# Second block's attention: units of two kinds mixed, heads paired across key groups, scores as three rounded products

## The reference

```python
proj = hn @ w_in                       # q_n, k_c, v_c, k_s, v_s, k_w, v_w, g_n, q_w, k_sw, v_sw
qn = rope(q_n)                         # 8 heads of 64: 2 key groups of 4 heads
k_c, k_s, k_w = rope(...)              # 2 key heads of 64 each
ckv = compress([k_c, v_c])             # 31 compressed keys and values of each key head
o_cmp, p_cmp = compressed_attention(qn, ckv[0], ckv[1], t)
o_slc = selected_attention(qn, k_s, v_s, idx, t)        # all 8 blocks of 64 keys, causal
o_win = banded_attention(qn, k_w, v_w, 512, None)       # 512 of 512 keys: causal
o_nsa = g0 * o_cmp + g1 * o_slc + g2 * o_win; o_nsa = rms_norm(o_nsa)
qw, kw = rope(q_w), rope(k_sw)         # 8 more heads, 2 key groups
o_swa = banded_attention(qw, kw, v_sw, 128, sinks); o_swa = rms_norm(o_swa)
mixed = concat([o_nsa, o_swa]) @ w_out
```

## Time and profile before

| | us |
|---|---|
| median of 3 runs | 1889.32 (1887.1 to 1889.44) |
| profiled execution | 1890.05 |
| its span, first to last instruction | 1888.2 |
| PE busy | 1825.2 (97%) |
| DVE busy | 1332.4 (71%) |
| ACT busy | 975.0 (52%) |

### The profile page before, as it was taken

The page is one execution under the profiler, slowest core; times in us unless marked ns, Lnnn a source line. Parts: engine busy times, 40 slices in busy tenths (PEclk is TensorE's granted clock), DMA queues, the critical chain, the costliest instruction groups (busy, mean ns, idle before and its releaser), DMA issues.

```text
span 1888.2 us, 26991 instructions
## 1 busy us (share of the span) xinstructions
PE 1825.2 (97%) x8975; PEld 1451.8 (77%) x8975; DVE 1332.4 (71%) x1885; ACT 975.0 (52%) x1550; POOL 190.9 (10%) x135
## 2 busy tenths in 40 slices
PE   6999999999999998999999999999898999999998
PEld 5775788888888875688888888887556678888887
DVE  6989777777655899867777755687675567777544
ACT  5468764444433458764444433576665554444322
POOL 0100120000133200020000033200021300000111
PEclk9999999999999999999999999999999999999999
DMA  6220233333233420133333233442000223332332
GB/s 168 71 80 1 65 92 100 93 96 97 77 99 99 109 73 23 33 91 99 90 100 100 72 97 99 109 143 79 12 1 12 78 78 100 91 98 86 89 95 76
DMA packets 285096, 154.46 MB, mean 82 GB/s; under 512 B 16949, under 2 KB 283095, under 8 KB 285015
## 3 DMA queue, kind: packets, MB, share of 16 engines
q1 hardware_dynamic: 284596, 153.26, 28.2%
q10 hardware_dynamic: 419, 0.17, 0.0%
HBM read 151.31 MB, written 2.10 MB: 81 GB/s over the span
## 4 chain that ended last, share of the span: by engine, by line
PE 79%; DVE 9%; issue 6%; ACT 6%; DMA 0%; DVEq 0%; SPq 0%; ACTq 0%
PE bank L575 24%; PE bank L576 24%; PE bank L577 24%; DVE cacc L1770 3%; PE bank L1019 1%; DVE nmax L1837 1%; PE bank L975 1%; PE bank L996 1%; ACT pr L1544 1%; DVE nmax L2071 1%; DVE w_lo L1630 1%; ACT w_hi L1177 1%; ACT pt L1560 1%; DMA x_in<-in_x 0%; PE bank L1091 0%
## 5 line engine op out<-in xcount | busy, mean ns | idle before, releaser
L575 PE MATMUL bank<-h_hi,w_hi 128*128 128x512 f32 x1448 | 571.7, 395 | 6.9 <-DVE w_lo L1630 6.7
L576 PE MATMUL bank<-h_lo,w_hi 128*128 128x512 f32 x1448 | 565.6, 391 | 0.0
L577 PE MATMUL bank<-h_hi,w_lo 128*128 128x512 f32 x1448 | 565.2, 390 | 0.0
L1177 ACT ACTIVATE w_hi<-raw 128x1024 fp32r<-128x1024 f32 (+3 forms) x314 | 312.0, 1000 | 488.2 <-PE bank L577 484.0
L1630 DVE TENSOR_TENSOR w_lo<-raw,w_hi 128x1024 fp32r<-128x1024 f32 (+3 forms) x314 | 375.4, 1201 | 230.9 <-ACT w_hi L1177 230.2
L575 PEld LDWEIGHTS bank<-h_hi,w_hi 128*128 128x128 f32 x1448 | 273.2, 189 | 69.7 <-issue 7.6
L576 PEld LDWEIGHTS bank<-h_lo,w_hi 128*128 128x128 f32 x1448 | 273.4, 189 | 57.8 <-issue 2.2
L577 PEld LDWEIGHTS bank<-h_hi,w_lo 128*128 128x128 f32 x1448 | 273.1, 189 | 57.3
L575 PE MATMUL bank<-a_hi,w_hi 128*128 128x512 f32 x528 | 206.1, 390 | 0.0
L577 PE MATMUL bank<-a_hi,w_lo 128*128 128x512 f32 x528 | 205.5, 389 | 0.0
L576 PE MATMUL bank<-a_lo,w_hi 128*128 128x512 f32 x528 | 205.4, 389 | 0.0
(11 more groups left out here) (317 smaller groups left out, 2258.4 us busy)
## 6 DMA issues: line engine op xcount, KB each, us to landing
raw<-in_w_up SPq DMA_DIRECT2D x132, 512.0 KB, 3.8
raw<-in_w_in SPq DMA_DIRECT2D x39, 512.0 KB, 4.0
raw<-in_w_down SPq DMA_DIRECT2D x48, 384.0 KB, 3.2
raw<-in_w_down SPq DMA_DIRECT2D x48, 320.0 KB, 3.0
raw<-in_w_o SPq DMA_DIRECT2D x16, 512.0 KB, 3.5
raw<-in_cmp_w SPq DMA_DIRECT2D x8, 512.0 KB, 3.9
raw<-in_w_out SPq DMA_DIRECT2D x8, 512.0 KB, 3.4
raw<-in_w_uq SPq DMA_DIRECT2D x8, 288.0 KB, 3.0
```

The source lines that it names most:

```text
L575: mm(o, wh, mh, start=start, stop=False)
L576: mm(o, wh, ml, start=False, stop=False)
L577: return mm(o, wl, mh, start=False, stop=stop)
L1177: last = A_(dst(w_hi), src(raw), ACT.Copy)
```

## The change

- Heads are paired across key groups: pair c holds heads c and c+4, so the two row halves have different key heads. Keys lie once (128 partitions, one add in `rope`), and the q slabs and w_out's slabs are loaded in two DMAs each. The norms' gains, gates, sinks and value columns follow the new pairing.
- Scores: queries and keys are split into high parts (ScalarE, `qk_high`) and low parts (VectorE, `qk_low`), and each unit makes three rounded products on the row halves. `HIGH_SLAB`, `LOW_SLAB`, `HIGH_UNIT` and `LOW_UNIT` place the splits.
- Order: two long units lead, then window units and long units of pairs 0 and 1 alternate; pairs 2 and 3 follow as before. Window chunks and the last long chunk use bank 7, the others bank 6. A sink column is made only when the bank doesn't hold it yet.
- Compressed branch: keys padded from 31 to 32, key heads in a block-diagonal `kcT` and `vcn`: 16 full-array score matmuls instead of 32 on halves, 16 transposes instead of 32, four ScalarE copies instead of eight, one output matmul a unit instead of two.

```diff
-UNITS = nsa_units(0) + nsa_units(1) + [(SC_SWA, c, t) for c in range(PAIRS) for t in range(NT)] + nsa_units(2) + nsa_units(3)
-CHUNKS = [(SC_WIN, 0), (SC_WIN, 1)] + [(SC_SWA, c) for c in range(PAIRS)] + [(SC_WIN, 2), (SC_WIN, 3)]
+def mixed_units(lead):
+
+    nsa, swa = nsa_units(0) + nsa_units(1), [(SC_SWA, c, t) for c in range(PAIRS) for t in range(NT)]
+    pairs = [unit for both in zip(swa, nsa[lead:]) for unit in both]
+    return nsa[:lead] + pairs + swa[len(nsa) - lead:]
+
+
+UNITS = mixed_units(2) + nsa_units(2) + nsa_units(3)
+CHUNKS = [(b, c) for b, c, t in UNITS if t == NT - 1 and b != SC_SLC]
+O_BANK = {chunk: 7 if chunk[0] == SC_SWA or chunk == (SC_WIN, 3) else 6 for chunk in CHUNKS}
...
+def sink_new(u):
+
+    return UNITS[u][0] == SC_SWA and (u < 2 or UNITS[u - 2][:2] != UNITS[u][:2])
...
+HIGH_SLAB = {4: ("ks", 0), 5: ("kw", 0), 6: ("kx", 0), 11: ("qx", 0)}
+LOW_SLAB = {5: ("ks", 0), 6: ("kw", 0), 7: ("kx", 0), 11: ("qn", 0), 12: ("qx", 0)}
+HIGH_UNIT = {4: ("qx", 1), 8: ("qn", 1), 12: ("qx", 2), 18: ("qx", 3), 22: ("qn", 2), 30: ("qn", 3)}
+LOW_UNIT = {5: ("qx", 1), 10: ("qn", 1), 13: ("qx", 2), 19: ("qx", 3), 23: ("qn", 2), 31: ("qn", 3)}
...
+                    load(G2, p, slot(p, KD, P)[:, :, 0:HD2], d_in2[:, :, c:c + HD2])
+                    sp.dma_start(slot(p, KD, P)[:, :, HD2:P], d_in2[:, :, c + PAIRS * HD2:c + (PAIRS + 1) * HD2])\
+                        .then_inc(q2_ready[i - (len(T_ORDER) - 2 * PAIRS)], 16)
...
+                    for c in range(PAIRS):
+                        o = (t % 2 * PAIRS + c) * 2 * NCP
+                        last = mm(C_B[t // 2][:, o:o + 2 * NCP], q_sum[:, 0, c, t * P:(t + 1) * P], kcT[:, :], start=True, stop=True)
...
             def turn_between(k):
-                for n in ((), (0,), (1,), (2,), (3,), (4,), (5,), (6, 7))[k]:
-                    cmp_turned(n)
+                if 3 <= k < 3 + NT:
+                    cmp_turned(k - 3)
...
-                for e in range(2):
-                    mm(o[e][:, c0:c0 + n * P], q[half(e), c, t * P:(t + 1) * P],
-                       k2[k][half(e), c // (PAIRS // KV2), k0 * P:(k0 + n) * P], start=True, stop=False)
+                for qs, ks in ((high_of, high_of), (high_of, low_of), (low_of, high_of)):
+                    for e in range(2):
+                        mm(o[e][:, c0:c0 + n * P], qs[q][half(e), t * P:(t + 1) * P], ks[k][half(e), k0 * P:(k0 + n) * P],
+                           start=qs is high_of and ks is high_of, stop=False)
...
-                    if b == SC_SWA and t < 2:
-                        last = mm(o[e][:, 2 * P:2 * P + 1], eye, sinks[:, 2 * c + e:2 * c + e + 1], start=True, stop=True)
+                    if sink_new(u):
+                        last = mm(o[e][:, 2 * P:2 * P + 1], eye, sinks[:, c + PAIRS * e:c + PAIRS * e + 1], start=True, stop=True)
...
-                if i == 1 and t == 0:
-                    pe.wait_ge(sw_done.sem, len(ROPED))
-                if t == 0 and i >= 2 and b != SC_WIN:
-                    pe.wait_ge(y_done.sem, y_done.at(N, i - 1))
+                if t == 0 and b != SC_WIN:
+                    if chunk_of(u) == (SC_SWA, 0):
+                        pe.wait_ge(sw_done.sem, len(ROPED))
+                    for n_ahead in banked_ahead(u):
+                        pe.wait_ge(y_done.sem, y_done.at(N, n_ahead))
...
+            def qk_high(name, c):
+                act.wait_ge(rope_done.sem, [r[:2] for r in ROPED].index((name, c)) + 1)
+                A_(high_of[name, c], sum_of[name, c], ACT.Copy).then_inc(qk_hi.sem, 1)
...
+                if s in HIGH_UNIT:
+                    qk_high(*HIGH_UNIT[s])
                 if s == 5:
                     copied(len(T_ORDER) - 1)
...
-                else:
-                    outs = [(k2[kind][o * 64:(o + 1) * 64, hd, :], slice(hd * 64, (hd + 1) * 64))
-                            for hd in range(KV2) for o in range(2)]
...
+            def qk_low(name, c):
+                dve.wait_ge(qk_hi.sem, SPLIT_ORDER.index((name, c)) + 1)
+                v.tensor_tensor(low_of[name, c], sum_of[name, c], high_of[name, c].bitcast(f32), ALU.subtract)\
+                    .then_inc(qk_lo.sem, 1)
...
+                if s in LOW_UNIT:
+                    qk_low(*LOW_UNIT[s])
                 if s == 6:
                     rope(len(ROPED) - 1)
```

More of the change, by code:

```diff
@@ L82 @@
 ROPED = [("kc", 0, 512), ("ks", 0, 768), ("kw", 0, 1024), ("kx", 0, 1816)] + \
[L83 removed]
+    [("qn", j, j * HD2) for j in range(4)] + [("qx", j, 1304 + j * HD2) for j in range(4)]
 T_ORDER = [("vc", 0, 640)] + ROPED
@@ L894, in cmp_keys @@
                 for m in range(2):
-                    last = mm(bank[4][:, 0:2 * NC], w2k[:, m, :], hid[:, m, :], start=m == 0, stop=m == 1)
+                    last = mm(bank[4][:, 0:2 * NCP], w2k[:, m, :], hid[:, m, :], start=m == 0, stop=m == 1)
                 last.then_inc(kv_mm.sem, 1)
@@ L900, in cmp_values @@
                 pe.wait_ge(sw_done.sem, 9)
-                for v in range(KV2):
-                    for m in range(2):
-                        last = mm(bank[1][0:NC, v * HD2:(v + 1) * HD2], hid[:, 2 + m, v * NC:(v + 1) * NC], w2v[:, m, :],
-                                  start=m == 0, stop=m == 1)
+                for m in range(2):
+                    last = mm(bank[1][0:2 * NCP, 0:HD2], hid[:, 2 + m, :], w2v[:, m, :], start=m == 0, stop=m == 1)
                 last.then_inc(kv_mm.sem, 1)
@@ L1495, in _ @@
                     act.wait_ge(kv_mm.sem, 2)
-                    A_(vcn[0:NC, :], bank[1][0:NC, 0:KV2 * HD2], ACT.Copy).then_inc(kv_done.sem, 1)
+                    for e in range(2):
+                        A_(vcn[e * NCP:(e + 1) * NCP, e * HD2:(e + 1) * HD2], bank[1][e * NCP:(e + 1) * NCP, 0:HD2],
+                           ACT.Copy).then_inc(kv_done.sem, 1)
+                    qk_high("qn", 0)
                 if p < S2_O - 1:
@@ L1523, in _ @@
                     act.wait_ge(kv_mm.sem, 1)
-                    A_(kcT[:, :], bank[4][:, 0:2 * NC], ACT.Copy).then_inc(kv_done.sem, 1)
+                    act.wait_ge(flat_done.sem, 2)
+                    for e in range(2):
+                        A_(kcT[e * HD2:(e + 1) * HD2, e * NCP:(e + 1) * NCP], bank[4][e * HD2:(e + 1) * HD2, e * NCP:(e + 1) * NCP],
+                           ACT.Copy).then_inc(kv_done.sem, 1)
                 if (kind, i) == ("c", 7):
@@ L1962, in rope @@
-                for o, part in outs:
-                    last = v.tensor_tensor(o, tz[part, 2, :], tz[part, 3, :], ALU.add)
-                last.then_inc(rope_done.sem, 1)
+                out = kc_rot[:, :] if kind == "kc" else sum_of[kind, j]
+                v.tensor_tensor(out, tz[:, 2, :], tz[:, 3, :], ALU.add).then_inc(rope_done.sem, 1)
                 dve.wait_ge(rope_done.sem, r + 1)
             def cmp_front():
-                mask = const[:, K_CMP:K_CMP + NT * NC].rearrange("p (t o c) -> p t o c", t=NT, o=1).to_broadcast([P, NT, PAIRS, NC])
@@ L2040, in _ @@
                     v.reciprocal(gates[:, :], gates[:, :]).then_inc(gate_done.sem, 1)
+                if kind == "t" and i in LOW_SLAB:
+                    qk_low(*LOW_SLAB[i])
                 if kind == "t" and 5 <= i < 5 + KD:
```

196 lines of the change are left out of this document (115 added, 81 removed).

## The result

The changed kernel takes 1906.86 us (median of 4 runs, 1905.14 to 1909.98), the kernel before 1888.56 beside it: ratio 1.010, 95% interval 1.008 to 1.012. It is 18.3 us slower, and the time lies above the range given. Its profiled execution took 1909.98 us, 3.1 above its median.

What follows compares the result with a forecast made beforehand. TensorE, busy 97% of the span, was taken as the bound. Sinks -0.8, last slab -0.7, scores and slabs -(2.4+0.8), start +0.9, order +6.0 and waits +0.5 gave +2.7 on 1889.32: 1892.0 us, range 1882.5 to 1898.5.

Steps and rivals of the forecast that it cites:

- +6.0 for the order: Attention units: waits, copies and subtractions in the mixed order cost 6.6 us, against 0.6 in the old order.
- gain in the last slab: Last slab: fewer transposes and ScalarE copies finish PE 2.5 us earlier, but VectorE is late next; gain 0.7 us.
- the sinks: Attention units: sink matmuls in five units instead of eight, about 0.26 us of PE each; -0.8 us.
- Slabs and last slab without splits: Ahead of the units: fewer VectorE adds and smaller compressed branch, split work left out; gains 1.0 and 2.1 us.
- Scores as three products: Unit scores: three one-pass rounded products replace two fp32 passes for each head; -2.4 us, 0.5 lost to waits.
- C: Unit scores: rounded matmuls of 128 columns run as plain fp32 does; +3.7 us, 1895.7, chance 0.10.
- D: Unit scores: rounded products of the two row halves do not run at once; +18.6 us, 1913, chance 0.08.
- L: Unit scores: weight loads are not hidden in the row halves; +4.7 instead of -2.4 us, 1899.1, chance 0.03.
- Splits: High and low parts of queries and keys: 0.2 and 1.4 us ahead of the units, 1.6 in them; +3.2.
- Order with its fewer sinks: Attention units: mixed-order waits 4.4 us and start of the units 0.9, less 0.8 for sinks; +4.5.
- the wait in step 5: Start of the units: PE waits 4.6 us for the last q slab's copies to leave bank 7; before, 2.90.
- Rival E: PE's waits bring one more 1.2 GHz stretch of 6 us, about 3 us lost; 1895, chance 0.13.

Runs made afterwards that it cites:

- a_arena: Changed kernel with the arena moved by 128 bytes, so that its distance from the weights is again a multiple of 256 bytes; 1890.36 us.
- b_arena: Kernel before with only the arena moved by 128 bytes, to its address in the changed kernel; 1901.56 us.
- a_old_fp32: Changed kernel with the arena realigned, the old unit order, and plain float32 scores without high and low parts; 1882.41 us.
- a_old_prods: Changed kernel, arena realigned, old unit order, three rounded products kept but made from one rounded tile each, without splits; 1883.85 us.
- a_old: Changed kernel with the arena realigned and the old order of the units, rounded scores kept; 1888.72 us.
- a_lead6: Changed kernel, arena realigned, with six long units ahead of the mixed ones instead of two and splits placed to fit; 1889.75 us.
- a_spread: a_lead6 with the last q slab's five copies one in each of steps 4 to 8 and its rotation in step 10; 1890.06 us.

## Why the prediction was wrong, point by point

**The step that failed is one that isn't there.** The sum took "the change part by part" and stopped at the second block's attention. That `const` grows by four columns stands in the diff, and I gave it no price. It moved the arena by 128 bytes, and that is 16.5 of the 18.3 us (a_arena); 13 of them are the start distance of 2160 matmuls. For the other 3.5 I have only an observation: the three kernels with a distance of 128 bytes have two stretches at 1.2 GHz between 700 and 760 us (PEclk 0.94 there; 0.97 with 64 bytes, 1.00 without), each about 1.7 us of loss, and in the units of its profiled execution the changed kernel was some 38 us at that level, a_arena some 31. But b_arena has the same two stretches and costs 13.4 in all, so these parts can't simply be added, and the rest stays open.

**The sum gave 1892.0, and with the address undone (a_arena) it is 1890.4.** That looks like a good forecast and is luck: its terms were off by more than the result, and cancelled. To compare them with the runs they have to be sorted as the runs sort them. The sum's +6.0 for the order holds 1.6 for copies and subtractions of the splits, and its gain in the last slab had 1.4 taken off for two more; the sinks belong to the order. Sorted so, the four parts are -3.1, -1.9, +3.2 and +4.5, together the same +2.7. Measured they are -5.8, +1.4, +4.9 and +1.6.

- *Slabs and last slab without splits: -3.1 forecast (1.0 and 2.1), -5.8 measured* (a_old_fp32, with pairing and the block-diagonal compressed branch). Some 3.4 of it may be clock: in its trace the kernel before has 3.4 us at 1.2 GHz at 1289, behind the compressed scores, and 3.4 at 1419, each a loss of half its length, and a_old_fp32 has neither. The first is missing in all twelve traces with the new compressed scores and there, between 1287 and 1311 us, in all five with the old ones; the second comes and goes. Up to the first maximum the traces bear the forecast out: from 1170 us, where both still run the same program, a_old_fp32 gets there 4.6 us sooner than the kernel before, 1.7 of it clock and 2.9 left.
- *Scores as three products: -1.9 forecast (-2.4, and 0.5 for waits that it brings), +1.4 measured.* Rivals C, D and L fall by the rows of the timeline above: the two halves start together, at one tile the three products start 0.16 and 0.11 us apart and are done after 0.48, and at four tiles they take 0.90, where L has 1.07, and 0.97 even without its 0.10 for a drain, which no run shows. By that, the Trainium skill's rule in the page "TensorE: Matmul & The Clock Gate", Part 3 ("What overlaps and what doesn't"), that loads overlap only matmuls of another row group, does not hold here: the loads of 1362.82 go to the same halves as the matmuls that start at 1362.82, and the next start 0.24 us later, so the loads took no time of their own. So the price of the instructions was right, and what it is worth was not. With the products the clock went down 10 us sooner: a_old_prods has 20 us at 1.2 GHz in its units, a_old_fp32 7, and the 6.8 us that this can cost are more than the 2.4 that the products were to save. That the clock is the whole difference is not shown.
- *Splits: +3.2 forecast, +4.9 measured* (a_old against a_old_prods), a difference within the doubt. Ahead of the first maximum they cost 1.6 us in the trace, as forecast (0.2 and 1.4). In the units the traces differ by 2.5 with equal time at 1.2 GHz, forecast 1.6; 1.2 of it are the subtractions in steps 23 and 31. The 0.9 between the traces and the medians I can't place.
- *Order with its fewer sinks: +4.5 forecast (4.4 and 0.9 less 0.8), measured +1.6* (with plain scores +4.2). The waits of the values came as worked out, 5.4 us more in steps 0 to 31 against 5.3, and the wait in step 5 as well. What failed, if the medians are right, is the step from waits to time: where a_lead6 and a_spread removed the largest wait, nothing was gained. That a wait in one unit was room for VectorE and ScalarE in the next is my reading, and not shown.
- *Rival E, one more stretch at 1.2 GHz*, was the mechanism nearest to what the unit stage did, and its size was off: it had 6 us at that level on top of the 6 seen, and the profiled execution has some 28 more in the units than the kernel before.

The range failed for one reason alone: nothing in it stood for a part of the program that the change leaves alone.

## What to carry to other kernels

When a kernel changes size anywhere in its memory plan, compare the start distance of the same matmuls in a part that wasn't touched, before any reasoning on the part that was; pin the addresses of operands that meet in a matmul instead of letting them follow from what lies ahead. A saving on the busiest engine is worth what the step's bound lets through: here VectorE was busy for nearly all of two window steps in four, in one of them slowed beside GpSimd, and two products of three gave back 0.36 of 0.94 us at full clock. Look at the granted clock of every execution too: here rounded products came with more time at 1.2 GHz. And removing the longest wait of a pipelined stage may gain nothing, as it did here; try it before counting it.
